# Input norm in two column halves beside the first two products, bias rows' products with them, and the Toeplitz transfers from two queues, in a two-block model kernel

## The reference, cut to what matters

```python
xn = rmsnorm(x, attn_norm_g)              # x * rsqrt(mean(x*x) + 1e-6) * g
proj = xn @ w_in                          # pool, dilated qkv, stick-breaking qkv, s5 input
...
b_bar = ((lam_bar - 1.0) / lam)[:, :, None] * b_t         # lam_bar = exp(lam * dt), 32 groups x 64 states
bu = jnp.einsum('gpc,bsgc->bsgp', b_bar, uf)
_, h = lax.associative_scan(combine, (a, bu), axis=1)
y = jnp.real(jnp.einsum('gcp,bsgp->bsgc', c_t, h)) + d_skip * uf
y = gelu(y); gl = y @ w_glu; y = gl[..., :512] * sigmoid(gl[..., 512:])
...
buckets = t5_bucket(jnp.clip(dist_sub, 0, band) * dil)    # dilated attention
bias = bias_tab[buckets]                                  # 12 heads, one row of 384 distances each
```

## Time and profile before

| | us |
|---|---|
| median of 3 runs | 3575.17 (3573.9 to 3576.09) |
| the profiled execution | 3572.89 |
| its span | 3571.2 |
| PE busy | 3412.1 (96%) |
| DVE busy | 1965.6 (55%) |
| ACT busy | 1356.3 (38%) |
| POOL busy | 461.3 (13%) |

### The profile page before, as it was taken

The page is one execution under the profiler, slowest core; times in us unless marked ns, Lnnn a source line. Parts: engine busy times, 40 slices in busy tenths (PEclk is TensorE's granted clock), DMA queues, the critical chain, the costliest instruction groups (busy, mean ns, idle before and its releaser), DMA issues.

```text
span 3571.2 us, 39536 instructions
## 1 busy us (share of the span) xinstructions
PE 3412.1 (96%) x16130; PEld 2770.9 (78%) x16130; DVE 1965.6 (55%) x2371; ACT 1356.3 (38%) x1880; POOL 461.3 (13%) x325
## 2 busy tenths in 40 slices
PE   7999999999899899999999999999899989999998
PEld 4778887877777578888888877777698768888886
DVE  7454452233554434687773264444576678888335
ACT  3232112333145733433331146353545454444213
POOL 0000000000001000344540010000000035554000
PEclk9999999999999999999999999999999999999999
DMA  3213241112410013233238322120203312333732
GB/s 111 61 38 123 97 165 60 48 48 81 139 51 27 27 51 112 95 112 111 107 122 320 112 83 92 59 100 30 95 1 124 118 71 106 113 112 140 309 105 83
DMA packets 114390, 353.82 MB, mean 99 GB/s; under 512 B 16009, under 2 KB 25993, under 8 KB 114193
## 3 DMA queue, kind: packets, MB, share of 16 engines
q1 hardware_dynamic: 114208, 351.28, 28.1%
HBM read 268.15 MB, written 81.91 MB: 98 GB/s over the span
## 4 chain that ended last, share of the span: by engine, by line
PE 82%; DVE 8%; ACT 7%; issue 1%; DMA 1%; SPq 0%; ACTq 0%; DVEq 0%
PE PS L491 41%; PE PS L2334 21%; PE PS L474 8%; PE PS L3678 1%; PE PS L1817 1%; PE PS L3690 1%; PE PS L2809 1%; ACT whi L431 1%; DVE wlo L436 1%; PE PS L1526 1%; ACT dS L1580 1%; PE PS L503 1%; PE PS L918 1%; PE PS L1839 1%; PE PS L509 1%
## 5 line engine op out<-in xcount | busy, mean ns | idle before, releaser
L436 DVE TENSOR_TENSOR wlo<-raw,whi 128x1024 fp32r<-128x1024 f32 (+3 forms) x393 | 499.1, 1271 | 443.9 <-ACT whi L431 441.3
L431 ACT CAST whi<-raw 128x1024 fp32r<-128x1024 f32 (+3 forms) x393 | 372.4, 948 | 745.4 <-PE PS L491 337.1
L491 PE MATMUL PS<-xhi,whi 128*128 128x512 f32 x1904 | 617.6, 406 | 32.5 <-DVE xlo L525 12.8
L491 PE MATMUL PS<-xlo,whi 128*128 128x512 f32 x1904 | 594.7, 394 | 0.0
L491 PE MATMUL PS<-xhi,wlo 128*128 128x512 f32 x1904 | 592.2, 392 | 0.0
L491 PEld LDWEIGHTS PS<-xhi,whi 128*128 128x128 f32 x1904 | 355.3, 191 | 123.5 <-issue 28.6
L491 PEld LDWEIGHTS PS<-xlo,whi 128*128 128x128 f32 x1904 | 362.2, 190 | 78.0
L491 PEld LDWEIGHTS PS<-xhi,wlo 128*128 128x128 f32 x1904 | 361.5, 190 | 77.8
L2334 PE MATMUL PS<-tf,whi 128*128 128x512 f32 x936 | 288.2, 389 | 1.7 <-DVE wlo L436 1.7
L2334 PE MATMUL PS<-xhi,whi 128*128 128x512 f32 x624 | 243.8, 391 | 7.2 <-DVE xlo L2319 5.6
L2334 PE MATMUL PS<-xlo,whi 128*128 128x512 f32 x624 | 243.5, 390 | 0.0
(11 more groups left out here) (553 smaller groups left out, 5554.2 us busy)
## 6 DMA issues: line engine op xcount, KB each, us to landing
raw<-in_w_up SPq DMA_DIRECT2D x88, 512.0 KB, 3.4
hid<-hs SPq DMA_DIRECT2D x88, 512.0 KB, 3.6
raw<-in_w_in SPq DMA_DIRECT2D x67, 512.0 KB, 3.2
slot<-hid SPq DMA_DIRECT2D x56, 512.0 KB, 6.5
adr<-in_w_ada SPq DMA_DIRECT2D x48, 512.0 KB, 4.5
raw<-in_w_down SPq DMA_DIRECT2D x48, 512.0 KB, 3.5
raw<-in_w_gate SPq DMA_DIRECT2D x32, 512.0 KB, 3.3
merged<-hid SPq DMA_DIRECT2D x16, 512.0 KB, 12.8
```

The costliest lines, as they stand in the source:

```text
L431: act.e.copy(whis[i % RING][:, ks, :], raws[i % RING][:, ks, :]).then_inc(*give("w_hi", i))
L436: dve.e.tensor_tensor(wlos[i % RING][:, ks, :], raws[i % RING][:, ks, :], whis[i % RING][:, ks, :].bitcast(F32), ALU.subtract).then_inc(*g ...
L491: ins = pe.e.matmul(ps[:, h * 512:(h + 1) * 512], w[s][:, k, :], x[:, h * 512:(h + 1) * 512], start=(at == 0 and n == 0), stop=(at == kt - ...
```

## The change

1. The norm works on 512 tokens at a time (`half[0]`, `half[1]`). X is loaded by halves: first half, weight tiles 0 and 1, second half. PE sums the squares of half 0, then does half 0 of both first products step by step, two squares of half 1 behind each of the first four; then the three bias matmuls; then half 1 of both products.
2. `x_ss` takes pair 2 and no longer a pair of `dense`; the bias rows take pairs 3 and 2 and no longer `rows_ring`.
3. The constants `ident`, `BC`, `cpos` are loaded behind X; `hot`, `pen`, `relb` there too and no longer in `s5_sp`.
4. On DVE `s5_powers` is a generator: its first part runs ahead of the norm, its second part after the norm, tile 2's `wlo` and the bias adds. ACT loads the table of ln and exp ahead of the squares.
5. Slot "cl" has 13 steps instead of 10; so all later slots hold steps three further on, and the last slot, "glu", has 2 instead of 5.
6. The wait of DVE for `bsc` ahead of CL goes; ACT has it ahead of the Ks copies.
7. Mk is sent by two queues: four transfers from SP, four from ACT, behind its Ks copies.

```diff
         def input_sp(sp):
             sp.e.dma_start(V, A["vecs"]).then_inc(*land("c_vecs"))
+            for k in range(8):
+                sp.e.dma_start(X[:, k, half[0]], A["xT"][:, k, half[0]]).then_inc(*land(f"lane{k}", "x"))
+            load_weights(sp, 0)
+            load_weights(sp, 1)
+            for k in range(8):
+                sp.e.dma_start(X[:, k, half[1]], A["xT"][:, k, half[1]]).then_inc(*land(f"away{k}", "x", 1))
+            load_weights(sp, 2)
...
+            load_weights(sp, 3)
+            load_weights(sp, 4)
+            sp.wait_ge("bias_row", 2)
+            sp.e.dma_start(bsc, brow).then_inc(*land("bsc"))
+            load_weights(sp, 5)
...
         def input_pe(pe):
-            ps = psum.take(pe, dense, "x_ss", ("xn_rstd_ln",))
+            total = psum.take(pe, [2], "x_ss", ("xn_rstd_ln", 1))
...
+            for k in range(8):
+                squares(k, 0)
+            ring = [0, 1]
+            first = [opened(pe, ring, "w_in", 34 + n, ("s5_u", n)) for n in range(2)]
+            steps = [half_steps(pe, i, ps, XNH, 0, done=False) for i, ps in first]
             for k in range(8):
+                next(steps[0])
+                next(steps[1])
+                if k < 4:
+                    squares(2 * k, 1)
+                    squares(2 * k + 1, 1)
...
+            rows = psum.take(pe, [3], "bias", ("bias_row", 1))
...
+            rows = psum.take(pe, [2], "bias2", ("bias_row", 2))
...
+            drive([half_steps(pe, i, ps, XNH, 1) for i, ps in first])
 
         def input_act(act):
...
             for k in range(8):
-                act.wait_ge("xn_g", k)
-                hi_of(act, XH[0][:, k, :], xtmp[(8 + k) % 3], "xn_hi", k)
+                high(k, 0)
+                if k < 4:
+                    square(2 * k, 1)
+                    square(2 * k + 1, 1)
+                if k == 5:
+                    root(1)
+            weights_hi(act, 2)
+            for k in range(8):
+                high(k, 1)
...
         def input_dve(dve):
...
+            powers = s5_powers(dve)
+            next(powers)
+            weights_lo(dve, 0)
...
+            for hf in range(2):
+                dve.wait_ge("xn_rstd", hf)
+                for k in range(8):
...
+                    if (k, hf) == (1, 0):
+                        weights_lo(dve, 1)
+                low(7, hf)
+            weights_lo(dve, 2)
+            for g in range(3):
+                dve.wait_ge("bias_mm", g)
...
+            next(powers, None)
             s5_coefficients(dve)
...
-        SLOTS = [("cl", 10), ("k", 3), ("ks", 6)]
+        SLOTS = [("cl", 13), ("k", 3), ("ks", 6)]
...
-            for q in range(8):
-                sp.e.dma_start(Mk[16 * q:16 * q + 16, :, 16 * q:128], Ks[:, :, 0:128 - 16 * q]).then_inc(*land("s5_mk", q))
+            for q in range(4):
+                s5_rows(sp, q, "s5_mk")
...
         def s5_act(act):
...
             beside_act(act, "cl")
+            act.wait_ge("bsc")
...
+                if hf:
+                    act.wait_ge("s5_ks", 1, 1)
+                    act.wait_ge("s5_mzero")
+                    for q in range(4, 8):
+                        s5_rows(act, q, "s5_mk2")
                 beside_act(act, "ks" if hf else "k")
...
             beside_dve(dve, "cl")
-            dve.wait_ge("bsc")
...
-            dve.wait_ge("s5_mk", 7)
+            dve.wait_ge("s5_mk", 3)
+            dve.wait_ge("s5_mk2", 7)
```

More of the change, by code:

```diff
@@ new lines, in input_sp, with input_pe, squares @@
+            load_weights(sp, 4)
+            sp.wait_ge("bias_row", 2)
+            sp.e.dma_start(bsc, brow).then_inc(*land("bsc"))
+            load_weights(sp, 5)
+        def input_pe(pe):
+            total = psum.take(pe, [2], "x_ss", ("xn_rstd_ln", 1))
+            pe.wait_ge("c_ones")
+            def squares(k, hf):
+                pe.wait_ge("x_sq", k, hf)
+                pe.e.matmul(total[:, half[hf]], ones, xtmp[k % 3][:, half[hf]], start=(k == 0), stop=(k == 7)).then_inc(*give("x_ss", k, hf))
+            for k in range(8):
+                squares(k, 0)
+            ring = [0, 1]
+            first = [opened(pe, ring, "w_in", 34 + n, ("s5_u", n)) for n in range(2)]
+            steps = [half_steps(pe, i, ps, XNH, 0, done=False) for i, ps in first]
+            for k in range(8):
+                next(steps[0])
[3 more added lines that the diff above has]
+                    squares(2 * k + 1, 1)
+            pe.wait_ge("c_hot")
+            pe.wait_ge("c_relb")
+            rows = psum.take(pe, [3], "bias", ("bias_row", 1))
+            for g in range(2):
+                pe.e.matmul(rows[0:4, 512 * g:512 * g + 384], relb[:, 4 * g:4 * g + 4], hot[:, 384 * g:384 * g + 384], start=True, stop=True).then_inc(*give("bias_mm", g))
+            rows = psum.take(pe, [2], "bias2", ("bias_row", 2))
+            pe.e.matmul(rows[0:4, 0:384], relb[:, 8:12], hot[:, 768:1152], start=True, stop=True).then_inc(*give("bias_mm", 2))
+            drive([half_steps(pe, i, ps, XNH, 1) for i, ps in first])
@@ new lines, in input_act, with square, root, high @@
+        def input_act(act):
+            act.e.preload_act_table_set("natural_log_exp_and_others")
+            def square(k, hf):
+                act.wait_ge(f"away{k}", "x", 1) if hf else act.wait_ge(f"lane{k}", "x")
+                if k >= 3:
+                    act.wait_ge("x_ss", k - 3, hf)
+                act.e.activation(xtmp[k % 3][:, half[hf]], X[:, k, half[hf]], ACT.Square).then_inc(*give("x_sq", k, hf))
+            def root(hf):
+                act.wait_ge("x_ss", 7, hf)
+                inverse_root(act, xrstd[:, half[hf]], psum.of("x_ss")[:, half[hf]], T, ("xn_rstd", hf), tables=False)
+            def high(k, hf):
+                act.wait_ge("xn_g", k, hf)
+                hi_of(act, XH[0][:, k, half[hf]], xtmp[k % 3][:, half[hf]], "xn_hi", k, hf)
+            for k in range(8):
+                square(k, 0)
+            weights_hi(act, 0)
+            root(0)
+            weights_hi(act, 1)
+            for k in range(8):
+                high(k, 0)
[7 more added lines that the diff above has]
+                high(k, 1)
@@ L671, in s5_powers @@
             ts(tau, th, 1.0 / (2 * math.pi), None, ALU.mult)
+            yield
             ts(t1, th, 0.25, None, ALU.mult)
@@ L853, in s5_pe @@
             pA, pB = [2], [3]
[L854 to L860, removed]
             beside("cl")
```

59 lines of the change are left out of this document (19 added, 40 removed).

## The result

| | before | changed |
|---|---|---|
| median of 7 runs each | 3575.17 us | 3589.53 us (3582.62 to 3592.69) |
| ratio | 1 | 1.0037, 95% interval 1.0027 to 1.0046 |
| profiled execution | 3572.89 (span 3571.2) | 3586.7 (span 3585.0) |
| PE busy | 3412.1 | 3416.9 |

The account below looks back on a forecast made before the run. PE is busy 96% of the span, so only its idle time in the first 350 us counts. 1.1 - 2.2 - 2.1 + 4.1 + 2.2 + 5.5 = +8.6 on 3572.89, plus 2.3 for the median: 3583.8 us; 8-in-10 range 3574 to 3589.

Parts of the forecast that it names:

- up to bu of half 0 (+1.1 and -2.2): First turned W starts at 118.3 against 117.30, +1.1; no idleness in front, so full clock, -2.2.
- up to L884: Half 1 of s5: the turned block at 184.40 no longer waits for DVE's `U`, -2.1.
- up to bu of half 1: A sigmoid waiting for the earlier gate's spill stands ahead of the WT copies; PE idles ahead of bu, +4.1.
- w_glu: First w_glu product takes pair 0, held by the last gate until its sigmoid ends at 272.50, not 267.00: +5.5.
- What becomes of the 15 us: PE's 15 us lead after the first two products is lost to DVE's gapless queue; K0 gains nothing.
- the sum of DVE's queue: DVE from its last `xlo` of half 0 (37.3) through CL of half 0: 41.1 of work, ending 78.4; before 78.7.
- Mk: Two queues carry Mk in 12 us, taken between 9.3 and 15.6; landed at 114.3, W ready at 118.1.
- the third rival: Two queues bring nothing: Mk takes 15.6, W ready at 121.7, PE idles 3.4 more; 3587.2 us; chance 0.13.
- Three in turn as before; I count nothing for them: Products after the first w_glu one take other pairs, but three in turn as before; counted as 0.
- the clock stays up: Clock does not fall in the idles before half 0 and bu; each saves 2.1 to 2.2; 3579.5 us; chance 0.20.
- pair 0 hidden: At w_glu the sigmoid comes earlier or the spill is not in its way; +3.1, 3578.3 us; chance 0.12.
- the head start arrives: PE's pace in half 0 does not hold DVE back; whole is -4, down to 3567 us; chance 0.10.

Follow-up runs that it names:

- e6_powers: Changed kernel with the second part of the powers cut in four and put into DVE's waits in half 0 of the norm; 3580.59 us.
- e5_kdve: Changed kernel with DVE's low part of weight tile 64 behind CL of half 1 instead of between the two halves; 3580.31 us.
- e11_cl10_pair: Changed kernel with 10 steps in slot "cl" and the shared list of PSUM pairs rotated, both as before; 3571.77 us.
- e2_memset: Changed kernel with GpSimd's clearing of Mk made to wait for CL of half 0 too; 3585.0 us.
- e4_mk_sp: Changed kernel with all 8 transfers of Mk from SP and none from ACT; 3589.56 us.
- e3_gate: Changed kernel with ACT's sigmoids of the gates and its copies of the w_in products two steps later in the table; 3584.68 us.
- e1_pair: Changed kernel with the shared list of PSUM pairs rotated once behind x_ss, as it was before; 3586.88 us.
- e12_mk_first: e9_ks9 with the weight load that waits for the low part of tile 64 behind Mk's transfers in SP's program; 3547.57 us.
- e8: e7_all with all 8 transfers of Mk from SP; 3559.52 us.
- e9_ks9: e8 with 9 steps in slot "ks", gates and spills later, SP's Mk transfers ahead of its slot "k"; 3553.03 us.
- e7_all: Changed kernel with the edits of e1_pair, e2_memset, e5_kdve and e6_powers, and 11 steps in slot "cl"; two queues for Mk; 3560.19 us.
- e10_ks9_two: e9_ks9 with four of Mk's transfers from ACT; 3552.88 us.

## Why the prediction was right, and where it was wrong

The direction was right, and so were three of the places where PE waits and their lengths; the size was 5.2 us short in the profile and 5.7 in the medians. That it was no shorter is partly luck: at the first bu the forecast lacked 8.0 us, and 2.1 came back behind w_glu for no reason that it gave. By its own steps, in the profile (changed minus before; the first row is a time, 81.70 before):

| step | forecast | measured |
|---|---|---|
| start of K of half 0 | 78.4 | 81.97 |
| up to bu of half 0 (+1.1 and -2.2) | -1.1 | +6.87 |
| up to L884 | -2.1 | -2.46 |
| up to bu of half 1 | +4.1 | +4.49 |
| clock behind it | +2.2 | +1.67 |
| w_glu | +5.5 | +5.31 |
| behind w_glu | 0 | -2.1 |
| sum | +8.6 | +13.8 |

- **What becomes of the 15 us** held: DVE's chains eat them. e6_powers and e5_kdve each gave 9 us back when one of the two chains went, and in e11_cl10_pair nothing of the 15 us reaches K of half 1. The third step of the chain, K of half 1 behind `wlo_64`, was forecast 16.0 behind K of half 0 (78.4 to 94.4) and is 16.28.
- **The failed step is the sum of DVE's queue, 37.3 + 41.1 = 78.4.** I added it up as if nothing could hold it, and did not follow what the earlier `bsc` releases on POOL. The queue starts on time (its last `xlo` of half 0 ends at 37.5) and takes 44.2 us; one tensor_scalar beside the memset makes 3.4 of that, and e2_memset takes them away. K of half 0 is 3.6 later than forecast, nearly all of it by this, out of the 8.0 us that the first bu lacks. The sentence "So K0 gains nothing" doesn't follow from its numbers: 78.7 is where CL ended before, but PE started K there at 81.70, so by its own sum K of half 0 would have come 3.3 earlier. That it gained nothing (81.97) is the memset's doing: in e2_memset it starts at 77.96.
- **Mk** was mis-sized: 12 us taken between 9.3 and 15.6; it is 15.3. The nearest row was the upper end, and the third rival had the term right; its total, 3587.2, comes near the median by luck, since it knows nothing of the memset. The rule of the page "DMA: Bandwidth & Descriptors" of the Trainium skill that the prediction cites and does not use had it right too: 15.1 to 15.4 us with two queues that start together, 15.0 to 15.7 with one. That is another 3.3. ACT's four issues were to cost nothing up to 7 us: they took 10.09 and made an idleness of 3.53, and e4_mk_sp shows that without it PE waits 3.25 for W instead and the time is the same. The rest, 1.1, is PE that reaches the first turned W (126.22) 1.6 after it is ready, behind that idleness and a granted clock of 0.63 (117.80 to 121.80), less small differences.
- **L884, the gate, w_glu** came within 0.4 us each, the clock behind the gate's idleness within 0.6; e3_gate confirms the gate and e1_pair the pair at w_glu. No run puts the wait at L884 back.
- **"Three in turn as before; I count nothing for them" failed**, and times that differ behind 360 us, one of the prediction's own signs of being wrong, came true. Counted from before at the same instruction, the changed kernel is 15.1 us late at 372.41, 14.6 at 731.80, then 16.2, 11.8, 10.3, again 14.8 at 1067.52, and 13.8 at the end. Two of these places go with the list in all profiles. From 1002.67 to 1021.08 (times of before) the six changed kernels without the rotation lose 2.9 to 3.1 us, those with it nothing but for e12_mk_first (1.5). At 2851.28 it is the other way round: those with the rotation lose 2.5 to 2.7 (rows at e1_pair), those without it at most 0.6. The gain of 5.8 in the changed kernel between 790 and 952 is 0 in e1_pair and 2.2 to 6.2 in the other kernels, with the rotation and without; its cause stays open, and so does the spread of the changed kernel's runs (10 us against 5 before).
- Of the rivals, "the clock stays up" fell (the granted clock is 0.61 over the 4.00 us behind the 3.71 at 20.12, and 0.68 over the 5.38 behind the 4.19 at 207.12), and "pair 0 hidden" and "the head start arrives" fell too.

```profile
20.12:24.12 4.00, 4.00 (x9) 2.79 (x10) 2.92 (x4) 1.23 (x3) 0.00 (x0) 0.61 1.04 384
72.41:77.41 5.00, 5.00 (x12) 3.94 (x13) 4.93 (x4) 0.00 (x0) 0.00 (x0) 0.50 0.65 210
...
207.12:212.50 5.38, 5.38 (x65) 5.21 (x65) 5.21 (x6) 2.22 (x2) 0.00 (x0) 0.68 0.00 0
```

(Stretches of the changed kernel, columns as in the earlier trace rows.)

## What to carry to other kernels

When an early stage gets faster, write down for every engine, GpSimd too, what its next instruction waits for, and place it anew: each thing released earlier (a memset, a load, a sigmoid) lands beside other work or ahead of something that was not in its way. A table of slots by step number moves the work of four engines at once; after such a shift read each engine's order around the two or three waits that set the time, and part the tables if one engine wants another place. And first find the engine whose chain is full: here 8.4 us of small instructions moved into DVE's waits gave 8.9 us (the memset's 3.4 among them), while the rearrangement of PE without that gave 2.6 (e11_cl10_pair), and that not through the norm.

## What the runs showed of the hardware that I had not expected

- A tensor_scalar of 128x16 that starts with GpSimd's memset of 128x4096 takes 3.59 us for 0.17, and one that starts shortly before its end takes 0.30 (e6_powers); tensor_tensor beside the same memset takes its usual time.
- Two queues that send the eight parts of Mk together need 15.1 to 15.4 us from the first issue to the first use (changed, e1, e2, e3, e5, e6), one queue 15.0 to 15.7 (before, e4, e8, e9, e12). ACT's four issues take 10.1 us while SP issues too, and 4.36 when SP does not (e7_all, e10_ks9_two, e11_cl10_pair).
- Behind 2.55 us of idleness ahead of the first turned W the granted clock was 0.58 over 2.71 us (eight transposes in 1.58 us, e9_ks9), behind the 2.25 us at 2862.73 of e1_pair 0.68 over 5.30; behind the 0.82 us ahead of the second turned W of e12_mk_first it was 1.00 over 2.31 (eight transposes in 1.07).
